# Query up-projection stores through a second staging buffer, gate rows loaded between weight pieces, two steps of the first stage moved

## What is computed

```python
mod_x = (sc_ @ w_ada[l] + b_ada[l])[:, None, :]          # 2048 -> 6 * 2048: shifts, scales, gates
sh1, s1, g1, sh2, s2, g2 = jnp.split(mod_x, N_MOD, axis=-1)
h = _modulate(_rmsnorm(x, norm1_w[l]), sh1, s1)
hc = _modulate(_rmsnorm(xc, norm1_w[l]), sh1c, s1c)
# _mixer_inputs: p = h @ w_in; q_da, k_da, v_da and two latents, then
q_mla = heads(c_q @ w_uq, MLA_HEADS)                      # 384 -> 1536, tokens of x only
kv = heads(c_kv @ w_ukv, MLA_HEADS)                       # 256 -> 2048, tokens of x and context
o_da = _sweep(lambda qb: _diff_attend(qb, k_da_all, v_da_all, lam), q_da)
o_mla = _sweep(lambda qb: _softmax_attend(qb, k_mla_all, v_mla_all, MLA_SCALE), q_mla)
x = x + g1 * (_merge_heads(o_da, o_mla, subln_w[l], lambda_init) @ w_o[l])
h2 = _modulate(_rmsnorm(x, norm2_w[l]), sh2, s2)
x = x + g2 * _conv_ffn(h2, w_up[l], conv_w[l], conv_b[l], w_down[l])
```

## Time and profile before

| | |
|---|---|
| median of three runs | 3104.43 us (3098.81, 3104.43, 3111.1) |
| the profiled execution, its own time | 3106.44 us |
| span of the profiled execution (first to last instruction) | 3104.4 us |
| mean granted clock of TensorE | 0.969 |
| PE busy | 2892.0 us (93%) |
| DVE busy | 1799.9 us (58%) |
| ACT busy | 1197.7 us (39%) |
| POOL busy | 167.8 us (5%) |
| moved by DMA | 617.54 MB, mean 199 GB/s |

### The profile page before, as it was taken

How to read it: one execution, slowest core, us unless ns; L and a number is a source line. 1 busy time by engine, 2 the same in 40 slices (tenths; PEclk the granted TensorE clock), 3 DMA queues, 4 the chain that set the end, 5 groups by cost and what they waited for, 6 DMA issues and landing times.

```text
span 3104.4 us, 34899 instructions
## 1 busy us (share of the span) xinstructions
PE 2892.0 (93%) x13848; PEld 2364.8 (76%) x13848; DVE 1799.9 (58%) x2014; ACT 1197.7 (39%) x1144; POOL 167.8 (5%) x344
## 2 busy tenths in 40 slices
PE   6899899898999999997999999989689999999997
PEld 3587775677888888886877888878677888888886
DVE  2387677665655455554455568956754554455553
ACT  2232226524454334344245434324333344344333
POOL 0000105000000000000000000026200000000000
PEclk9899999999999999999899999999899999999999
DMA  9598874564555665555357776674145555665553
GB/s 395 205 330 287 301 270 161 211 235 163 189 176 169 203 223 169 183 173 181 115 176 241 232 228 220 213 227 117 45 142 177 179 186 168 202 203 185 173 173 132
DMA packets 347856, 617.54 MB, mean 199 GB/s; under 512 B 51760, under 2 KB 102592, under 8 KB 340304
## 3 DMA queue, kind: packets, MB, share of 16 engines
q1 hardware_dynamic: 310848, 582.82, 56.0%
q10 hardware_dynamic: 36880, 32.94, 3.2%
HBM read 586.70 MB, written 29.00 MB: 198 GB/s over the span
## 4 chain that ended last, share of the span: by engine, by line
PE 81%; DVE 10%; DMA 4%; ACT 3%; issue 2%; SPq 1%; POOL 0%; ACTq 0%; DVEq 0%; POOLq 0%
PE ps L306 21%; PE ps L308 21%; PE ps L307 21%; DVE w_lo L269 3%; PE ps L1012 3%; PE ps L1014 3%; PE ps L1013 3%; PE ps L1294 1%; DMA g_row<-in_w_ada 1%; DVE upd L2278 1%; PE ps L617 1%; PE ps L2576 1%; ACT w_hi L262 1%; PE ps L387 1%; DMA raw<-in_pack_ada 1%
## 5 line engine op out<-in xcount | busy, mean ns | idle before, releaser
L269 DVE TENSOR_TENSOR w_lo<-raw,w_hi 128x2048 fp32r<-128x2048 f32 (+3 forms) x428 | 892.1, 2094 | 694.8 <-ACT w_hi L262 693.5
L262 ACT ACTIVATE w_hi<-raw 128x2048 fp32r<-128x2048 f32 (+3 forms) x428 | 745.1, 1753 | 798.6 <-PE ps L308 703.1
L306 PE MATMUL ps<-w_hi,a_hi 128*128 128x512 f32 (+1 forms) x2272 | 891.5, 392 | 17.0 <-DVE a_lo L656 6.8
L307 PE MATMUL ps<-w_lo,a_hi 128*128 128x512 f32 (+1 forms) x2272 | 884.9, 389 | 0.0
L308 PE MATMUL ps<-w_hi,a_lo 128*128 128x512 f32 (+1 forms) x2272 | 884.9, 389 | 0.0
L306 PEld LDWEIGHTS ps<-w_hi,a_hi 128*128 128x128 f32 x2272 | 430.7, 190 | 109.6 <-DVE a_lo L656 8.6
L308 PEld LDWEIGHTS ps<-w_hi,a_lo 128*128 128x128 f32 x2272 | 430.8, 190 | 88.9
L307 PEld LDWEIGHTS ps<-w_lo,a_hi 128*128 128x128 f32 x2272 | 431.0, 190 | 85.9
L306 PE MATMUL ps<-w_hi,b_hi 128*128 128x512 f32 x864 | 341.4, 395 | 18.6 <-DVE w_lo L269 13.5
L307 PE MATMUL ps<-w_lo,b_hi 128*128 128x512 f32 x864 | 339.7, 393 | 0.0
L308 PE MATMUL ps<-w_hi,b_lo 128*128 128x512 f32 x864 | 339.5, 393 | 0.0
(11 more groups left out here) (327 smaller groups left out, 2756.3 us busy)
## 6 DMA issues: line engine op xcount, KB each, us to landing
raw<-in_hyb_w_in SPq DMA_DIRECT2D x96, 1024.0 KB, 5.5
raw<-in_sc_w_in SPq DMA_DIRECT2D x96, 1024.0 KB, 5.2
raw<-in_w_up SPq DMA_DIRECT2D x88, 1024.0 KB, 5.1
raw<-in_pack_ada SPq DMA_DIRECT2D x96, 512.0 KB, 6.0
raw<-in_w_down SPq DMA_DIRECT2D x48, 768.0 KB, 4.4
raw<-in_w_in SPq DMA_DIRECT2D x24, 1024.0 KB, 7.4
raw<-in_hyb_w_out SPq DMA_DIRECT2D x32, 768.0 KB, 4.5
raw<-in_sc_w_out SPq DMA_DIRECT2D x32, 768.0 KB, 4.5
```

The source lines that it names most:

```text
L262: nc.scalar.activation(w_hi[s][:, 0:n_k, 0:ncols], raw[s][:, 0:n_k, 0:ncols], ACT.Copy).then_inc(sem("hi_done"), 1)
L269: nc.vector.tensor_tensor(w_lo[s][:, 0:n_k, 0:ncols], raw[s][:, 0:n_k, 0:ncols], w_hi[s][:, 0:n_k, 0:ncols].bitcast(F32), ALU.subtract).th ...
L306: nc.tensor.matmul(o, h, w_hi[s][:, k, 0:ncols], start=kt == 0, stop=False)
L307: nc.tensor.matmul(o, h, w_lo[s][:, k, 0:ncols], start=False, stop=False)
```

## The change

1. First stage: of piece 1's four steps, the last two come after blocks 24 and 25 and no longer after 22 and 23.
2. Projection: the second and the fourth `uq` chunk get the kind `ur`: DVE copies them into `stg[1]`, and ACT only waits for that copy and issues the DMA; they count as stores from `stg[1]` (`C_STORED`) and no longer from `stg[0]`. The stores of all eight short chunks stand one piece earlier on ACT and DVE (`stored_at`): ahead of the split of piece e+2 where the chunk ends with piece e-1.
3. Output projection: for chunks 1 to 3 SP loads pieces 0 and 1, the first row of the second gate, pieces 2 and 3, and the second row.

```diff
-            step_after = dict(zip((15, 16, 17, 18, 20, 21, 22, 23, 27, 28, 29, 30), steps))
+            step_after = dict(zip((15, 16, 17, 18, 20, 21, 24, 25, 27, 28, 29, 30), steps))
...
-            *[("uq", W_UQ, n * UQ_N, UQ_N, False, PQ) for n in range(4)], ("in", W_IN, OFF_K + CHUNK, CHUNK, True, PROJ),
+            *[(("uq", "ur")[n % 2], W_UQ, n * UQ_N, UQ_N, False, PQ) for n in range(4)], ("in", W_IN, OFF_K + CHUNK, CHUNK, True, PROJ),
...
+        SHORT = ("uk", "uq", "ur")
+
+        def stored_at(j):
+
+            return ENDS[j] + (2 if CHUNKS[j][0] in SHORT else 3)
...
-        X_STORED = [sum(ch[5] is not None for ch in CHUNKS[:j]) for j in range(len(CHUNKS) + 1)]
-        C_STORED = [sum(ch[4] for ch in CHUNKS[:j]) for j in range(len(CHUNKS) + 1)]
+        X_STORED = [sum(ch[5] is not None and ch[0] != "ur" for ch in CHUNKS[:j]) for j in range(len(CHUNKS) + 1)]
+        C_STORED = [sum(ch[4] or ch[0] == "ur" for ch in CHUNKS[:j]) for j in range(len(CHUNKS) + 1)]
...
+            if kind == "ur":
+                act.wait_ge(*proj_free(c))
+                act.dma_start(tok(dst[:, c0:c0 + w]), stg[1][:, :, 0:w]).then_inc(sem("stored_c"), 16)
+                return
...
         def store_dve(dve, j):
-            _, _, _, w, both, _ = CHUNKS[j]
-            c = ACC[j] + 1
-            if both:
+            kind, _, _, w, both, _ = CHUNKS[j]
+            c = ACC[j] + both
+            if both or kind == "ur":
...
-                    if ENDS[j] + 3 == p:
+                    if stored_at(j) == p:
...
-                if n:
-                    load_chunk(sp, WO, n, n * CHUNK)
-                    for kt in range(G2_ATT + 2 * n, G2_ATT + 2 * n + 2):
-                        g2_load(sp, kt)
+                for g, (kt, n_k) in enumerate(WO.groups if n else ()):
+                    load_piece(sp, WO, WO.p0 + n * WO.per + g, kt, n_k, n * CHUNK)
+                    if g % 2:
+                        g2_load(sp, G2_ATT + 2 * n + g // 2)
```

More of the change, by code:

```diff
@@ L693, in build_program @@
             ("in", W_IN, 0, CHUNK, False, PROJ_X), *[("uk", W_UKV, n * CHUNK, CHUNK, True, PKV) for n in range(4)],
-            *[("uq", W_UQ, n * UQ_N, UQ_N, False, PQ) for n in range(4)], ("in", W_IN, OFF_K + CHUNK, CHUNK, True, PROJ),
+            *[(("uq", "ur")[n % 2], W_UQ, n * UQ_N, UQ_N, False, PQ) for n in range(4)], ("in", W_IN, OFF_K + CHUNK, CHUNK, True, PROJ),
             ("in", W_IN, CHUNK, CHUNK, False, PROJ_X), ("in", W_IN, OFF_V + CHUNK, CHUNK, True, PROJ))
         K0, QL, KL, V0, Q0 = range(5)
+        SHORT = ("uk", "uq", "ur")
+        def stored_at(j):
+            return ENDS[j] + (2 if CHUNKS[j][0] in SHORT else 3)
         ATT_FIRST = (30, 31, 33, 35)
-        UQ_LAST = max(j for j, ch in enumerate(CHUNKS) if ch[0] in ("uk", "uq"))
+        UQ_LAST = max(j for j, ch in enumerate(CHUNKS) if ch[0] in SHORT)
         GROUPS = {"in": k_groups(KT, 4), "lat_q": k_groups(KT, 4), "lat_kv": k_groups(KT, 4), "uk": [(0, KV_RANK // P)],
-                  "uq": [(0, Q_RANK // P)]}
+                  "uq": [(0, Q_RANK // P)], "ur": [(0, Q_RANK // P)]}
         PIECES = [(K0, 0), (K0, 1), (K0, 2), (QL, 0), (QL, 1), (K0, 3), (QL, 2), (QL, 3)] + [
@@ L980, in proj_acts @@
                 return [(tile_list(lat_hi, f), tile_list(lat_lo, f)) for f in (3, 5)]
-            if kind == "uq":
+            if kind in ("uq", "ur"):
                 return [(tile_list(lat_hi, 0), tile_list(lat_lo, 0))]
@@ L1001, in proj_piece @@
                     pe.wait_ge(sem("flip_lo"), 4 * (g + 1))
-                if kind in ("uk", "uq"):
+                if kind in SHORT:
                     pe.wait_ge(sem("flip_lo"), LAT0 + 7)
```

## The result

| | before | changed |
|---|---|---|
| median | 3108.77 us (5 runs, 3098.81 to 3111.1) | 3081.8 us (5 runs, 3070.58 to 3083.03) |
| ratio | | 0.9912, 95% interval 0.9888 to 0.9936 |
| the profiled execution, span | 3104.4 us | 3081.1 us |
| mean granted clock | 0.969 | 0.973 |

The change makes the kernel 0.9% faster, 27 us by this ratio. The same kernel was timed twice more beside the experiments, with ratios of 0.9927 and 0.9921, 23 and 25 us. The forecast was 3083 us.

The account below looks back on a forecast made before the run. PE, busy 2892.0 of 3104.4 us, was taken as the bound, so only its idle or low-clock time could be won. Gains 5.5 + 7.0 + 8.5 = 21.0 us gave 3083 us, range 3075 to 3096.

Parts of the forecast that it names:

- Part 1: First stage, before piece 2: an earlier column total makes the split ready sooner, leaving 1.5 of 6.97 us idle; gain 5.5.
- the term that stood as upper end: First step of piece 2: if 1.5 us of idling keep PE's clock up, another 2.4 us comes, 7.9 in all.
- Part 2: Projection, before K1: K1 starts 9.5 to 5.6 us earlier, middle 7.5; 7.0 taken as gain in time.
- the third chunk waits for the first store alone: Projection: with the second `uq` chunk in the other buffer, the stores let K1 start at 327.7 to 330.2 us.
- The other bound: Before K1: piece 28's load waits for the later split of piece 26, so it is ready at 331.6 us.
- DVE's reserve: Within K1: DVE's 9.30 us wait for PE's sum, less two added copies, leaves 6.9 us before PE waits.
- Part 3: Output projection: earlier gate rows close the gaps of 3.85 and 2.05 us and save 2.5 of clock; 8.5 taken.
- DMA engines set K1's start: Before K1: nearly full DMA engines leave only 2.2 us to the short chunks; time 3088 us, chance 17%.
- Row landing last: Output projection: the gate row lands with the pieces behind it, the change there gives 2; time 3090 us, chance 9%.
- More comes back: First stage and projection: `uk` chunks also shorten and the clock stays up at piece 2; gain 26.0, 3078 us, 10%.
- Slower, DVE waits for landings: Projection: six copies on DVE each wait for a store's landing, making PE wait; 24 us slower, 3128 us, 3%.
- Something fixed takes parts 1 and 2 back: Before attention: first-stage and short-chunk gains end at something fixed, such as late units; time 3096 us, chance 4%.

Follow-up runs that it names:

- e5: The changed kernel with the short chunks' stores back at their old place, one piece later, second buffer kept: 3087.91 us, ratio 0.995.
- e6: The changed kernel with all four `uq` chunks through `stg[0]` again, the earlier stores kept: 3084.02 us, ratio 0.9937.
- e4: The changed kernel with two late units moved from after piece 35 to after piece 39: 3088.14 us, ratio 0.9954.
- e1: The kernel before with only the two steps of piece 1 moved behind blocks 24 and 25: 3099.41 us, ratio 0.9986.
- e2: The kernel before with only the second staging buffer and the earlier place of the eight short stores: 3097.38 us, ratio 0.9976.
- third profile: The changed kernel with nothing altered, timed and profiled a third time: 3081.29 us, ratio 0.9921.
- a_again: The changed kernel with nothing altered, timed again beside other experiments: 3082.42 us, ratio 0.9927.

## Why the prediction came out right

The total was right, 3083 for 3081.8. The sum had 21.0 us; the stages give 22.8 to 24.3. Measured from piece 1 on, K1 starts 17.2 us earlier (231.00 for 248.15), where 13 were forecast, and attention 14.2, where under 12 was to be a sign of error. Parts 1 and 3 came by the mechanism that was forecast. In part 2 the size came right with a working that was half right, and so far that was luck.

**Part 1** said 5.5 and is worth 8.1. The mechanism held to the tenth: from the column total to the end of the split there were 10.50 us before (118.21 + 2.30 - 110.01) and now 10.51. The chain after:

```profile
102.29 1.00 PE ps L399 x8
...
110.50 2.30 DVE w_lo L792
```

Mis-sized was the term that stood as upper end: the clock. The windows of 10 us before and after (columns as in the earlier trace rows) show PE's granted clock around the start of piece 2, which was 120.65 and is 112.94:

```profile
120.00:130.00 10.00, 9.35 (x38) 6.74 (x39) 1.44 (x4) 1.49 (x1) 0.00 (x0) 0.73 0.30 97
```

```profile
110.00:120.00 10.00, 8.94 (x55) 5.36 (x55) 3.23 (x4) 1.89 (x2) 0.00 (x0) 1.00 0.79 290
```

The first step of piece 2 takes 3.0 us (112.94 to 115.95 in the chain) where it took 5.2. After an idle time of 1.06 us PE stays at 2.4 GHz, after 6.97 it was at 1.2. That is 2.2. The gap gives 5.9, and by the means of the stage the whole is 8.1; in this pair of profiles it is 8.7, since PE also came to piece 2 0.6 us sooner after piece 1. The sum should have held both, the gap and the clock: in all nine profiles with 1.05 to 1.08 us of idling there the clock stayed up. Whether the 1.5 us of the forecast would have left it there is not shown; 1.9 us at another place did so only in some profiles (last section).

**Part 2** said 7.5 at K1 and 7.0 in time. K1 came 8.7 earlier, and 0.7 are given back before attention. It took the second buffer for the cause and the earlier place for a cost, the load of piece 28 behind a later split. e5 and e6 show each half worth 4 to 5 us. The step that failed is the sentence that with the second buffer "the third chunk waits for the first store alone": it left out that ACT must wait for DVE's copy to issue its DMA, and that at the old place this wait of 6.84 us stands ahead of the third copy.

The other bound was the load of piece 28, K1's first. It is indeed the DVE half of that piece's split that releases K1, but the load did not set it. The load was issued at 305.47 (DMA issues of 304.5:306, median us to landing):

```profile
raw<-in_w_in SPq DMA_DIRECT2D x1, 1024.0 KB, 7.7
```

It had landed at 313.2, while ACT came to the split at 314.45, held by its wait for DVE's copy, which ended at 313.95. So here too it is ACT's order, and ahead of that the store whose landing ACT waited 5.10 us for. K1's gap is 0.73 us and not the 2 to 6 forecast, since PE had itself lost 2.54 us at the fourth `uq` chunk, whose split stands on ACT right behind those 5.10 us. The prediction named such a wait for piece 26 alone and set it at nothing.

DVE's reserve: its 9.30 us wait for PE's sum is gone, as forecast. The larger gap, 3.24 us before V1, was named as a sign of error, and it is one for the reserve: it was spent. The timeline of DVE ahead of V1's first split shows it waiting for the load of a late unit:

```profile
385.53 0.75 DVE L922 SCALAR_TENSOR_TENSOR run<-raw,condf,run 128x512 f32<-128x512 f32 x1 [3.90 <-DMA raw<-in_pack_ada]
```

K1 to V1 takes 70.72 us, against 70.34 before, so the gap itself cost little. The clock behind it cost up to 2.6: V1 to attention takes 57.4, 54.8 and 56.4 us in the three profiles of the change, and 54.8 before. e4 moved the wait and did not remove it, so the late units are close to being the next bound from K1 to attention; whether by their loads or by DVE's adds was not separated.

**Part 3** said 8.5. Against the profile before, three of the four profiles with it shown in the table give 7.4 (85.02 less 77.6) and the fourth 9.0. The difference is the clock after the gap that stayed, below: it was 1.00 before and in the fourth, 0.66 in the three, where the prediction had 1.00. With the same clock there it is 9.0 for before, 9.2 for e1 (86.83 less 77.6) and 11.6 for e2 (87.65 less 76.0). Both gaps closed, the 1.92 stayed, and DVE waits 0.95 us for the row.

**The rivals.** *DMA engines set K1's start*: fell. Part 2 was to give 2.2 us, and K1 came 8.7 earlier, while the DMA share there rose from 0.89 to 0.96 and PE was never idle:

```profile
320.00:340.00 20.00, 20.00 (x89) 16.55 (x89) 17.02 (x19) 4.46 (x4) 0.00 (x0) 1.00 0.96 325
```

The Trainium skill (DMA: Bandwidth & Descriptors, "Issuing engines are not separate DMA queues") says that DMAs of different engines run on the same 16 DMA engines and interleave. Single landings agree with it: the store that K1's chain goes through takes 7.63 us, where another of 512 KB took 3.5. So what fell is the rival's price. That the landings have no part in K1's start is not shown: e6 kept the order of the two stores and lost most of the gap as they landed sooner, and in the changed kernel one landing stands ahead of the 2.54 and 0.73 us that are left. *Row landing last*: fell, DVE's wait for it is 0.95 us. *More comes back*: part 1 did so. *Slower, DVE waits for landings*: the wait of 5.72 us in front of the copy is gone; in front of an earlier `uk` copy DVE waits 2.57 us for a landing, where before it waited 4.11. *Something fixed takes parts 1 and 2 back*: fell as a whole; only e2 shows something of it, the 1.9 us that its row's gaps took back in the output projection.

## What to carry to other kernels

A second buffer helps only as far as the orders of the copying and the issuing engine let it: look for the instruction that has to wait for the other engine's copy, for what stands ahead of that copy, and for what stands behind the wait. Count the clock with the gap: closing a gap of 7 us down to 1 gave 2.2 us more than the gap. A row that arrives last from a queue of large loads could here be pulled forward at no cost, since its consumers come in another order than its issue. Compare stages by their own lengths over several profiles: two profiles at one mark differ by up to 4 us from start-up on, and one stage by 1.6 us from the clock behind a gap that is the same in both.

## What the hardware showed beside

The same idle time does not always bring the same clock. In front of the second chunk of the output projection PE idles 1.88 us in the profile of the change and 1.90 in the third profile; the windows behind it read, first the one and then the other:

```profile
600.00:610.00 10.00, 8.12 (x29) 6.22 (x29) 9.90 (x11) 1.34 (x1) 0.00 (x0) 0.84 0.80 291
```

```profile
600.00:610.00 10.00, 8.11 (x36) 6.39 (x35) 9.90 (x11) 1.19 (x1) 0.00 (x0) 1.00 0.78 287
```

Once the clock was lower for a time, once it was not. All ten profiles with part 3 fall on two values of this stage, 77.61 to 77.65 us (five) and 76.02 to 76.05 (five), 1.6 us apart with nothing between. In the first five the clock of the 5 us behind that gap (1.88 to 1.91 us in all ten) is 0.66 to 0.68, in the others 1.00. Before V1 it is the same: after 3.24 us of idling the window 390 to 400 of the change has 0.75, after 3.10 that of a_again has 1.00, and V1 to attention takes 57.4 and 54.8 us. What decides it was not tested.
